# Seven block products for eight in 19 of 22 first-FFN tile pairs per layer, with four FFN blocks

## The reference

```python
h2 = rms_norm(x, p['g_pre_ffn']) * (1 + sc2) + sh2
gate, up = jnp.split(h2 @ p['w_ffn_in'], 2, axis=-1)
f = (jax.nn.silu(gate) * up) @ p['w_ffn_out']
x = x + g2 * rms_norm(f, p['g_post_ffn'])
```

## Time and profile before

| | |
|---|---|
| median of three runs | 2121.35 us |
| span of the profiled execution | 2119.3 us |
| whole time of the profiled execution | has no figure of its own; the median lies 2.05 us over the span |
| TensorE busy | 2091.1 us, 99% |
| GpSimd busy | 1215.9 us, 57% |
| VectorE busy | 694.4 us, 33% |
| ScalarE busy | 409.4 us, 19% |
| DMA | 211.03 MB, mean 100 GB/s |
| mean granted TensorE clock | 0.997 |

### The profile page before, as it was taken

One profiled execution on the slowest core, in us unless ns is written; L12 is line 12 of the kernel. 1 busy time (PEld: TensorE's weight loads), 2 busy tenths in 40 slices (PEclk: granted clock), 3 DMA queues, 4 the chain that ended last, 5 costly groups with the idle time before them and its releaser, 6 DMA issues.

```text
span 2119.3 us, 37755 instructions
## 1 busy us (share of the span) xinstructions
PE 2091.1 (99%) x16673; PEld 2019.9 (95%) x16673; DVE 694.4 (33%) x1223; ACT 409.4 (19%) x906; POOL 1215.9 (57%) x596
## 2 busy tenths in 40 slices
PE   8999999999999999999999999999999999999997
PEld 7999898999999999999999989899999999999997
DVE  5323556322354110011464236662215621001113
ACT  4111234110232100111222111331103311111111
POOL 0444454658753666677736445446686366666764
PEclk9999999999999999999999999999999999999999
DMA  9736222223253432422422443113234122222322
GB/s 359 268 115 63 67 64 60 73 80 100 80 167 123 157 108 83 130 80 84 166 62 66 60 65 81 54 57 83 80 100 159 51 71 83 72 85 82 88 69 86
DMA packets 298323, 211.03 MB, mean 100 GB/s; under 512 B 12544, under 2 KB 292656, under 8 KB 294960
## 3 DMA queue, kind: packets, MB, share of 16 engines
q1 hardware_dynamic: 291408, 205.08, 33.7%
q10 hardware_dynamic: 6752, 3.53, 0.9%
HBM read 203.80 MB, written 4.07 MB: 98 GB/s over the span
## 4 chain that ended last, share of the span: by engine, by line
PE 96%; DVE 1%; DMA 1%; ACT 1%; POOL 1%; issue 0%; SPq 0%; DVEq 0%; POOLq 0%; ACTq 0%
PE ps L801 65%; PE ps L826 13%; PE ps L845 3%; PE ps L851 2%; PE ps L969 2%; PE ps L893 1%; PE ps L1181 1%; PE ps L1346 1%; DMA raw<-in_w_in 1%; PE ps L1309 1%; PE ps L1196 1%; PE ps L1324 1%; PE ps L872 1%; PE ps L1376 1%; PE ps L1012 1%; PE ps L1275 0%
## 5 line engine op out<-in xcount | busy, mean ns | idle before, releaser
L801 PE MATMUL ps<-h_hi,hi_lo 128*128 128x288 f32 x5504 | 977.3, 297 | 0.2 <-ACT kall L1631 0.2
L749 POOL TENSOR_TENSOR hi_lo<-raw,consts 128x1024 fp32r<-128x1024 f32 (+2 forms) x258 | 462.4, 1792 | 765.1 <-PE ps L801 514.9
L801 PEld LDWEIGHTS ps<-h_hi,hi_lo 128*128 128x128 f32 x5504 | 814.8, 189 | 7.5 <-issue 5.3
L752 POOL TENSOR_TENSOR hi_lo<-raw,hi_lo 128x1024 fp32r<-128x1024 f32 (+2 forms) x258 | 599.8, 2325 | 20.2
L801 PE MATMUL ps<-h_lo,hi_lo 128*128 128x288 f32 x2752 | 589.4, 296 | 0.0
L801 PEld LDWEIGHTS ps<-h_lo,hi_lo 128*128 128x128 f32 x2752 | 443.7, 189 | 0.0
L826 PE MATMUL ps<-y_hi,hi_lo 128*128 128x288 f32 x1232 | 220.5, 298 | 0.9 <-POOL hi_lo L752 0.8
L1925 DVE TENSOR_TENSOR tmp<-sq,ps 128x576 f32<-128x576 f32 x44 | 33.2, 754 | 571.0 <-PE ps L801 562.9
L826 PEld LDWEIGHTS ps<-y_hi,hi_lo 128*128 128x128 f32 x1232 | 182.0, 189 | 2.5 <-POOL hi_lo L752 1.8
L826 PE MATMUL ps<-y_lo,hi_lo 128*128 128x288 f32 x616 | 131.8, 296 | 0.0
L1631 ACT ACTIVATE tmp<-ps 128x576 f32<-128x576 f32 x60 | 39.0, 651 | 380.5 <-PE ps L801 380.5
(11 more groups left out here) (344 smaller groups left out, 2356.5 us busy)
## 6 DMA issues: line engine op xcount, KB each, us to landing
raw<-in_w_in SPq DMA_DIRECT2D x108, 512.0 KB, 3.8
ada<-in_w_ada SPq DMA_DIRECT2D x23, 2048.0 KB, 9.2
raw<-in_w_ffn_in SPq DMA_DIRECT2D x88, 512.0 KB, 3.8
raw<-in_w_ffn_out SPq DMA_DIRECT2D x32, 384.0 KB, 3.4
raw<-in_w_ffn_out SPq DMA_DIRECT2D x32, 320.0 KB, 3.1
raw<-in_w_out SPq DMA_DIRECT2D x16, 512.0 KB, 4.0
...
```

The source lines that it names most:

```text
L749: pool.tensor_tensor(hi, RAW[s][:, 0:size], ONES[:, 0:1].to_broadcast([128, size]), ALU.mult).then_inc(chunk_hi, 1)
L752: pool.tensor_tensor(lo, RAW[s][:, 0:size], hi.bitcast(f32), ALU.subtract).then_inc(chunk_split, 1)
L801: m = pe.matmul(o[:, h, :], a[:, k, c0:c0 + 128], mv(k, h), start=(k == 0 and begins), stop=(k == nk - 1 and a is wl))
```

## The change

```diff
-BLOCKS = (11, 11)
+BLOCKS = (6, 5, 5, 6)
+NB, PLAINP = len(BLOCKS), 3
+PRODUCTS = ("p1", "p5", "p6", "p2", "p7", "p3", "p4")
...
@@ SyncE @@
+                def blocks_read(b, n):
+                    if b == "a11":
+                        sp.wait_ge(s_alo, 3 * n + 1)
+                    elif b == "a12":
+                        sp.wait_ge(s_alo, 3 * n + 2)
+                    elif b == "a22":
+                        sp.wait_ge(s_alo, 3 * n + 3)
+                    sp.wait_ge(s_sum, 4 * n + (4 if b == "a12" else 3))
...
+                        if (l, c, i) == (0, LASTB, 3):
+                            sp.wait_ge(s_prod, 7 * NSP)
                             for a in IN_P2[1]:
                                 part_load(sp, 1, a)
+                            for nm in (("cos", "sin"), ("sel", "sel")):
+                                x = slice(CO[nm[0]][0], CO[nm[1]][1])
+                                sp.dma_start(CST[:, x], A["consts"][:, x]).then_inc(tables_loaded, 16)
...
@@ GpSimd @@
+                def block_split(o, c, r):
+                    n = spairs(l, c) + r
+                    pool.wait_ge(s_raw[o], 16 * (n + 1))
+                    if r or o == "a11":
+                        if n:
+                            pool.wait_ge(s_prod, nth_product(n - 1, {"a11": "p1", "a12": "p2", "a22": "p4"}[o]))
...
+                for c in range(NB):
+                    if c == 0:
+                        pool.wait_ge(t_hi, nth(t_hi, l, 2))
+                        pool.tensor_tensor(T4L[:, :, :], T4SUM[:, :, :], T4H[:, :, :].bitcast(f32), ALU.subtract) \
+                            .then_inc(t_lo_pool, 1)
+                    block_split("a11", c, 0)
+                    block_split("a12", c, 0)
+                    for r in range(SPAIRS[c]):
+                        block_split("a22", c, r)
+                        if r + 1 < SPAIRS[c]:
+                            block_split("a11", c, r + 1)
+                            block_split("a12", c, r + 1)
+                    for i in range(8):
+                        out_split(c, i)
...
@@ TensorE @@
+                def product_begins(c, r, p):
...
+                    elif p == "p7":
+                        pe.wait_ge(s_lo, 4 * n + 3)
+                        pe.wait_ge(s_e, 3 * n + 3)
+                        if (c, r) == (0, 0):
+                            pe.wait_ge(t_lo, nth(t_lo, l, 2))
...
+                    else:
+                        pe.wait_ge(s_alo, 3 * n + 3)
+                        pe.wait_ge(s_c22, n + 1)
...
+                def product(c, r, p):
+                    wh, wl = OPND[WEIGHTS[p]]
+                    bh, bl = DATA[p]
...
+                    for k in range(4):
+                        for a, mv in ((wh, bh), (wh, bl), (wl, bh)):
+                            if k == 3 and a is wl:
+                                if i < 6:
+                                    product_begins(c, r, PRODUCTS[i + 1])
...
+                            m = pe.matmul(o, a[:, k * 128:(k + 1) * 128], mv(k), skip_group_check=True,
...
@@ ScalarE, h_hi @@
+                        if first:
+                            act.activation(MID[:, k, 0:SEQ], TS[:, k % 2, 0:SEQ], ACT.Identity, bias=MOD[:, part, k, 0:1])
+                            act.activation(MID[:, k, SEQ:T], TS[:, k % 2, SEQ:T], ACT.Identity, bias=MOD[:, part, k, 1:2]) \
+                               .then_inc(hf_ready, 1)
                         if k == 0 and (l, first) != (0, 0):
                             copy_r2(l, "n2b" if first else "n1b")
...
@@ VectorE @@
+                def gate_half(c, r):
+                    n = spairs(l, c) + r
+                    dve.wait_ge(s_prod, nth_product(n, "p7"))
+                    dve.wait_ge(s_e, 3 * n + 2)
...
+                    tt(C22[:, :], q1(l, c, r), E5[:, :], ALU.add).then_inc(s_c22, 1)
```

More of the change, by code:

```diff
@@ L205 @@
 P_FFN = P_WO + 8
-NCH = P_FFN + sum(2 * b + 16 for b in BLOCKS)
+P_FO = P_FFN + 2 * PLAINP
+NCH = P_FO + 8 * NB
 assert NCH % 2 == 0
@@ L263, in slots @@
     for l in range(DEPTH):
-        for p in range(NCH):
+        for p in range(P_FO):
             fresh = {}
@@ new lines, in blocks_read @@
+                def blocks_read(b, n):
[6 more added lines that the diff above has]
+                    sp.wait_ge(s_sum, 4 * n + (4 if b == "a12" else 3))
+                for j in range(PLAINP):
+                    for s in range(2):
+                        cols(s, P_FFN + 2 * j + s, w_fi, j * 128 + s * FFN)
@@ new lines, in _ @@
+                run_begins("fi0_4", P_FFN + 4)
+                feature_group("fi0_4", P_FFN + 4, 8, 128, 0, *HM, lead=True)
+                feature_group("fi0_5", P_FFN + 5, 8, 128, 0, *HM, lead=True, ahead=False)
+                product_begins(0, 0, "p1")
+                gm = tuple((lambda k, h, lo=lo: y_tile(lo, k)[:, h * HALF:(h + 1) * HALF]) for lo in (False, True))
+                j0 = 0
+                for c, nb in enumerate(BLOCKS):
+                    for r in range(SPAIRS[c]):
+                        for p in PRODUCTS:
+                            product(c, r, p)
@@ new lines, in _ @@
+                sum_high(1, 0, 0)
+                sum_high(2, 0, 0)
+                sum_high(3, 0, 0)
+                for c in range(NB):
+                    plain = PLAINP * (c == 0)
+                    for r in range(SPAIRS[c]):
+                        more = r + 1 < SPAIRS[c]
+                        if r:
+                            silu(0, c, r - 1)
+                        keep(0, c, r)
+                        if (c, r) == (0, 0):
+                            t_high(3, T3H, T3SUM)
+                        sum_high(4, c, r)
+                        if r:
+                            high_ys(c, r - 1, plain + r - 1)
+                        elif c == 0:
+                            high_y(PLAINP - 1)
+                        keep(1, c, r)
+                        keep(2, c, r)
+                        if more:
+                            sum_high(1, c, r + 1)
+                            sum_high(2, c, r + 1)
+                        silu(1, c, r)
+                        if more:
+                            sum_high(3, c, r + 1)
+                    silu(0, c, SPAIRS[c] - 1)
+                    high_ys(c, SPAIRS[c] - 1, BLOCKS[c] - 1)
+                    for i in range(8 if c < LASTB else 0):
+                        nm = f"fo{c}_{i}"
+                        if c == 0:
@@ L2547, in _ @@
+                for k in range(8 if l == DEPTH - 1 else 0):
                     post_tile("p2", k)
-                    if l == DEPTH - 1 and k:
+                    if k:
                         nm, c0 = f"gk{k - 1}", slice((k - 1) * 128, k * 128)
```

682 lines of the change are left out of this document (512 added, 170 removed), and 6 rows, old and new, of the table AFTER.

## The result

| | before | after |
|---|---|---|
| median of four runs | 2121.29 us (2120.98 to 2122.81) | 2094.19 us (2091.33 to 2095.31) |
| ratio | | 0.9869, 95% interval 0.9855 to 0.9883 |
| span of the profiled execution | 2119.3 us | 2091.6 us |

The change makes the kernel 27 us faster. The forecast was 2096 us, in a range of 2066 to 2119. First the page of after (busy time and granted clock), against the earlier trace rows.

What follows compares the result with a forecast made beforehand. TensorE, busy 99% of the span, was taken as the bound. Removing 60.8 us of matmuls and adding 4.2, 15.0, 2.1, 5.6, 5.4 and 3.0 gave -25.5, so 2096 us, in a range of 2066 to 2119.

Steps and rivals of the forecast that it cites:

- signs of being wrong: Pairs over 12 us apart mid-block, no stall at the entry, or the granted clock falling behind the stalls.
- Matmuls, -60.8: Projection pairs on TensorE: 96 matmuls become 84, 456 fewer at 133 ns each, 60.8 us less.
- that rival: Products do not run at 133 ns because operands change every 12 matmuls; at 143 ns, +32 us, 2128; chance 0.05.
- Steady pairs, +4.2: Pairs with a successor in their block: c22 late by 0.15 us at p4 in 28 pairs, +4.2 us.
- The ring as the bound: VectorE's ring limits every pair, at c22 and p4; at 2.4 us a pair, 2159 us, slower; chance 0.10.
- Entry, +15.0: FFN entry, first pair of each layer: operands late at p1, p5, p7 and c22, 7.5 us a layer, +15.0 us.
- T3's +2.4: FFN entry: T3's sum starts only after the plain tiles, so p7 waits, +2.4 us a layer.
- Copies of h, +2.1: FFN input: ScalarE's two copies into mid stand ahead of the row of root values, +1.05 us a layer, +2.1.
- Block ends, +5.6: Last pair's chain outlasts the first output tile: 0.9 us in four blocks of 5, 0.5 in four of 6, +5.6.
- Big loads, +5.4: Layer 0's last block: big loads and constants delay the fourth output tile's weights, +5.4 us.
- End of layer 0, +3.0: VectorE falls 1 to 2 us behind in the output tiles at layer 0's end; estimated +3 us.
- Rival "the clock falls": Slow clock after three long stalls (entries, big loads), 16 us, costs +8, about 2112; chance 0.13 shared with upper ends.

Runs made afterwards that it cites:

- run 8: Changed kernel with product p4 of every pair made of its last 3 matmuls, not 12 (result incomplete): 2055.52 us.
- run 3: Changed kernel reordered at the FFN's entry: GpSimd splits A11 before T4's low part, VectorE does S1 and S2 earlier: 2090.64 us.
- run 5: Changed kernel, entry reordered: GpSimd splits A11 and A12 before T4's low part, now four instructions; VectorE does S1, S2 and their low parts earlier: 2092.53 us.
- run 10: Changed kernel with run 5's entry order, and ScalarE, not GpSimd, making the high parts of A11, A12 and A22 in each layer's first pair: 2091.27 us.
- run 4: Changed kernel with ScalarE's copy of the row of root values ahead of its two copies of h into mid: 2093.68 us.
- run 1: Changed kernel with the big loads and constants in layer 0's last block issued ahead of output tile 6's weights, not tile 3's: 2085.25 us.
- run 9: Changed kernel plus 44 discarded matmuls on TensorE before the wait for the fourth output tile's weights in layer 0's last block: 2090.11 us.
- run 7: Meant to add 44 discarded matmuls to the changed kernel, but none were added, so the changed kernel a second time: 2092.51 us.
- run 2: Changed kernel without VectorE's addition of products to their running sum for output tiles 1 to 6 of layer 0 (result incomplete): 2086.86 us.
- run 12: Run 11 with ScalarE copying p1's half earlier, big loads and constants moved behind next-layer weight chunks, and those chunks split in halves: 2075.07 us.
- run 11: Changed kernel with run 10's entry, run 4's order, loads before output tile 7, layer 0's last output splits halved, next five chunks in thirds: 2078.72 us.

## Why the prediction was right

The mechanism and the sum held: 60.8 us out, 33.7 us back where 35.3 were forecast. Term by term it is less good: what I had too high for the pairs, the entry and the block ends is what I had too low for the end of layer 0 and for the clock. That the sum came within 2 us is luck. One of the prediction's own signs of being wrong, that the granted clock falls behind the stalls, came true as well.

- *Matmuls, -60.8.* Right: 456 fewer, 133 ns apart in the products. That the products have new operands every 12 matmuls costs nothing; that rival is out.
- *Steady pairs, +4.2.* Measured about 1 us, a single wait of 0.55 us for c22 at 952.78 and a few of 0.15. The step that failed is where I had A12's high part go ahead of S1. I had held gate times up, low S3 and y_lo longer than GpSimd held them, so S1 came first; run 8 shows 1 us more of slack in every pair. The ring as the bound, the slower rival, is out with it.
- *Entry, +15.0.* Measured 10.9. The places were right (p1 and p5, p7, p4) and T3's +2.4 was 2.9; p1 and p5 came to 2.0 where I had 3.4, and what p4 waited for was GpSimd's low part of A22, where I had c22; p1 too had GpSimd as releaser and not VectorE. Runs 3, 5 and 10 show that order moves the waits, and run 10 that they shrink with work taken from GpSimd; how much would be left with ScalarE's queue in a good order no run shows.
- *Copies of h, +2.1.* Measured +0.85 a layer, 1.7 in all (run 4): most of ScalarE's 1.05 us.
- *Block ends, +5.6.* Measured 1.7, in two of eight blocks: 0.85 and 0.87 us at the two of five hidden tiles in layer 1, for the 0.9 I had. The 0.5 for a block of six was a slip, as 4.1 less 4.0 is 0.1, and next to nothing is there. 0.9 us for weights in layer 0's second block (a wait of 0.7) was not foreseen.
- *Big loads, +5.4.* Measured 6.6, and 1.9 more by the clock (runs 1, 9). The working was right, the fall of the clock wasn't added.
- *End of layer 0, +3.0.* This is the mis-sized term: what the other terms leave of the 33.7 us is 33.7 - 1 - 10.9 - 1.7 - 2.6 - 8.5 = 9.0 us. The traces say the same over layer 0 alone: from h_lo to h_lo it was 1090.74 - 636.66 = 454.1 us before and is 449.9 now, with 30.4 us of matmuls gone, so 26.2 came back, and 26.2 - 5.5 (entry) - 1.2 (pairs) - 0.9 (weights) - 8.5 = 10.1; with run 7's 446.8 it would be 7. Run 2 gives 9.3 us back with one instruction per tile, and from the gather to the next stream TensorE takes 1084.36 - 1057.30 = 27.1 us, in run 12 1063.83 - 1045.67 = 18.2 (of which 3.5 are lost again at h_lo). I had put the lag at 1 to 2 us in all; it is 0.4 to 1.4 us per tile, since two instructions per tile are held up, and it ends in two waits of 3 us with a slow clock behind them.
- *Rival "the clock falls".* It had a price of 8 us and the wrong places: no fall behind the 2.9 us at the entry (window 686 to 690: 1.00), but behind the loads (1.9 us) and at the end of layer 0, there within the 9 to 10 us: ten sum matmuls take 1.1 us more, 12 of the last tile 1.5, twenty more sums at 1072.69 (window 1072.6 to 1076.5: 0.59) 1.5. As a mechanism it was real. Its 16 us of stalls were also too few by my own terms (2 x (3.4 + 2.4) + 5.4 = 17, with c22's 20.4).

Still open: why the clock fell behind 3.2 us without work at the gather and not behind 2.9 us at the entry. What differs is that at the gather ten small sum matmuls follow; no run took them apart. They are not needed for a fall: behind the stops of 4.5 and 4.1 us at the next layer's start in runs 11 and 12, which only 288-column matmuls follow, the clock was 0.50 and 0.53 for 3 us.
